# Four buffers of their own for the early modulation chunks, and a last norm on two engines instead of three

## What is computed

```python
h = jax.nn.gelu(einsum('tkd,td->tk', u, xx))      # PEER: all expert rows u against the tokens
mod = silu(c) @ w_ada + b_ada                      # 9 x 1024 modulation values, for x and for the context
x = x + 0.5 * g3x * swiglu(modulate(rmsnorm(x)), w13_ffn2, w2_ffn2)   # the last matmul is with w2_ffn2
return rmsnorm(x, norm_final)
```

## Time and profile before

| | us |
|---|---|
| median of 3 runs | 2147.66 (2146.67 to 2149.58) |
| the profiled execution: its own time | 2149.38 |
| its span in the profile | 2147.6 |
| PE busy in it | 2084.9 (97%) |
| DVE, ACT, POOL busy | 1233.9, 1037.9, 145.6 |
| mean DMA rate | 160 GB/s |

### The profile page before, as it was taken

How to read it: one execution, slowest core, us unless ns; L and a number is a source line. 1 busy time by engine, 2 the same in 40 slices (tenths; PEclk the granted TensorE clock), 3 DMA queues, 4 the chain that set the end, 5 groups by cost and what they waited for, 6 DMA issues and landing times.

```text
span 2147.6 us, 35688 instructions
## 1 busy us (share of the span) xinstructions
PE 2084.9 (97%) x12718; PEld 1820.1 (85%) x12718; DVE 1233.9 (57%) x2078; ACT 1037.9 (48%) x1585; POOL 145.6 (7%) x86
## 2 busy tenths in 40 slices
PE   8999999899999999999999999999999999999997
PEld 6899988668888888888888888887888898899996
DVE  5457895896666666666665333323655644356554
ACT  5645644675555555555554222213443444336763
POOL 1001667000000000000000000000000000000001
PEclk9999999999999999999999999999999999999999
DMA  5445456786655555565553223322333345354563
GB/s 203 152 131 174 148 206 216 256 309 209 192 191 186 186 189 188 190 205 186 189 165 106 93 95 97 108 97 83 97 100 118 101 145 176 100 186 144 177 197 117
DMA packets 95669, 343.97 MB, mean 160 GB/s; under 512 B 11011, under 2 KB 11523, under 8 KB 95333
## 3 DMA queue, kind: packets, MB, share of 16 engines
q1 hardware_dynamic: 94340, 337.28, 47.1%
q0 software_dynamic: 1248, 5.57, 0.8%
HBM read 341.76 MB, written 1.05 MB: 160 GB/s over the span
## 4 chain that ended last, share of the span: by engine, by line
PE 88%; DVE 4%; DMA 3%; ACT 2%; POOL 1%; issue 1%; SPq 0%; ACTq 0%; DVEq 0%; POOLq 0%
PE ps L1652 15%; PE ps L1653 15%; PE ps L1654 15%; PE ps L1911 8%; PE ps L1925 6%; PE ps L1927 5%; PE ps L1926 5%; PE ps L1913 4%; DMA RAW<-in_wstream 3%; PE ps L1685 2%; PE ps L1686 2%; PE ps L1687 2%; PE ps L1889 2%; POOL WL L458 1%; ACT WH L512 1%; PE ps L1847 1%
## 5 line engine op out<-in xcount | busy, mean ns | idle before, releaser
L993 DVE TENSOR_TENSOR WL<-RAW,WH 128x1024 fp32r<-128x1024 f32 x517 | 624.9, 1223 | 407.3 <-ACT WH L512 401.3
L512 ACT ACTIVATE WH<-RAW 128x1024 fp32r<-128x1024 f32 x565 | 585.5, 1053 | 280.2 <-PE ps L1927 106.7
L1652 PE MATMUL ps<-XH,WH 128*128 128x256 f32 (+1 forms) x1200 | 382.3, 319 | 6.0 <-DVE XL L1022 4.0
L1653 PE MATMUL ps<-XL,WH 128*128 128x256 f32 (+1 forms) x1200 | 379.1, 316 | 0.0
L1654 PE MATMUL ps<-XH,WL 128*128 128x256 f32 (+1 forms) x1200 | 379.1, 316 | 0.0
L1911 PE MATMUL ps<-XHL,WH 128*128 128x512 f32 x752 | 268.6, 397 | 0.0
L1652 PEld LDWEIGHTS ps<-XH,WH 128*128 128x128 f32 x1200 | 229.1, 191 | 24.7 <-DVE XL L1022 5.0
L1653 PEld LDWEIGHTS ps<-XL,WH 128*128 128x128 f32 x1200 | 229.3, 191 | 14.6
L1654 PEld LDWEIGHTS ps<-XH,WL 128*128 128x128 f32 x1200 | 229.2, 191 | 14.2
L1913 PE MATMUL ps<-XHL,WL 128*128 128x256 f32 x752 | 210.9, 280 | 0.0
L1925 PE MATMUL ps<-WH,AH 128*128 128x512 f32 x512 | 202.4, 395 | 0.0
(11 more groups left out here) (340 smaller groups left out, 3359.9 us busy)
## 6 DMA issues: line engine op xcount, KB each, us to landing
RAW<-in_wstream SPq DMA_DIRECT2D x637, 512.0 KB, 3.4
H<-in_xT SPq DMA_DIRECT2D x4, 256.0 KB, 6.1
CTX<-in_ctxT POOLq DMA_DIRECT2D x1, 1024.0 KB, 8.0
HX<-in_ctxT POOLq DMA_DIRECT2D x1, 1024.0 KB, 5.9
DIST<-in_dist POOLq DMA_DIRECT2D x1, 1024.0 KB, 5.4
out<-Y SPq DMA_DIRECT2D x4, 256.0 KB, 3.0
MASK<-in_mask POOLq DMA_DIRECT2D x1, 512.0 KB, 3.9
DFTL<-in_dftl POOLq DMA_DIRECT2D x1, 512.0 KB, 3.7
```

What stands on the lines that cost most here:

```text
L512: act.activation(WH[:, slot, :], RAW[:, slot, :], ACT.Copy).then_inc(hi_ready, 1)
L993: dve.tensor_tensor(WL[:, slot, :], RAW[:, slot, :], WH[:, slot, :].bitcast(F32), ALU.subtract).then_inc(lo_ready, 1)
L1652: pe.matmul(dst, wh, xh, start=start, stop=False, skip_group_check=not check)
L1653: pe.matmul(dst, wh, xl, start=False, stop=False, skip_group_check=not check)
```

## The change

The twelve early modulation chunks leave the stream and the ring. They stand at the end of the stream's array and are loaded into a buffer `ADB` of four slots in a free part of SBUF, with semaphores of their own. SP issues the first four with the loads of the stage before ("wq"), and the other eight with every second load of "pre"; `C_PRE` becomes contiguous.

The last four `down2` chunks are done for tile 0 first (chunk by chunk, both halves), then for tile 1 half 0 over the four chunks, then for tile 1 half 1. POOL's two steps of the last norm go to DVE, in a new order on DVE and ACT, and the fourth store is issued by ACT and not by SP.

```diff
-    ("ada", MODB),
+    ("ada", MODB - EARLY),
...
+C_PRE = range(C0["pre"], C0["pre"] + PRE)
+C_ADA = [None] * EARLY + list(range(C0["ada"], C0["peer"]))
...
+        ADB = sb("ADB", [P, 4, 1024])
...
+            def load_early(i):
+                if i >= 4:
+                    sp.wait_ge(s["early_used"], i - 3)
+                sp.dma_start(ADB[:, i % 4, :], a["wstream"][NCH + i]).then_inc(s[f"early_landed{i % 4}"], 16)
...
-            looped = C0["pre"] // 4
+            looped = C0["wq"] // 4
...
             for c in range(4 * looped, ADA_END):
-                if c in C_ADA:
+                if c >= C0["ada"]:
                     sp.wait_ge(chunk_done, c + 1)
                 else:
-                    sp.wait_ge(lo_ready, split_index(c) + 1)
+                    sp.wait_ge(lo_ready, c + 1)
                 load(c % 4, c + 4)
+                i = c - 4 * looped - 4
+                if 0 <= i < 4:
+                    if i == 0:
+                        sp.wait_ge(chunk_done, C0["wout"])
+                    load_early(i)
+                i = (c - C0["pre"] - 6) // 2 + 4
+                if (c - C0["pre"]) % 2 == 0 and 4 <= i < EARLY:
+                    load_early(i)
...
@@ mod_chunk (PE)
-                pe.wait_ge(landed[c % 4], 16 * (c // 4 + 1))
+                if i < EARLY:
+                    weights, used = ADB[:, i % 4, :], s["early_used"]
+                    pe.wait_ge(s[f"early_landed{i % 4}"], 16 * (i // 4 + 1))
+                else:
+                    weights, used = RAW[:, c % 4, :], chunk_done
+                    pe.wait_ge(landed[c % 4], 16 * (c // 4 + 1))
...
@@ down2 (PE)
             for k in range(FF):
-                c = C0["down2"] + k
-                split_ready(c)
+                split_ready(C0["down2"] + k)
                 pe.wait_ge(s["ffn_lo"], FF + k + 1)
-                for tt in range(TT):
+                for tt in range(TT if k < FF - 4 else 1):
                     for half in range(2):
...
-                if k < FF - 1:
+                        ins = down2(k, tt, half)
+                if k < FF - 4:
                     ins.then_inc(chunk_done, 1)
+            for half in range(2):
+                for k in range(FF - 4, FF):
+                    down2(k, 1, half)
...
@@ last norm (DVE)
             gated(0, 0)
+            added(0, 0)
             gated(0, 1)
+            added(0, 1)
+            dve.wait_ge(s["lastg_landed"], 16)
+            gain(0, 0)
+            half_mean(0)
+            gain(0, 1)
+            inverse(0)
             gated(1, 0)
-            added(0)
+            added(1, 0)
+            gain(1, 0)
+            half_mean(1)
             gated(1, 1)
-            added(1)
-            dve.wait_ge(s["lastg_landed"], 16)
-            half_mean(0)
-            half_mean(1)
-            gain(1)
-            inverse(0)
-            gain(0)
+            added(1, 1)
+            gain(1, 1)
             inverse(1)
...
@@ last norm (ACT)
             square(0, 0)
             square(0, 1)
             root(0)
+            scaled(0, 0)
+            scaled(0, 1)
             square(1, 0)
             square(1, 1)
             root(1)
-            scaled(0, 0)
-            scaled(0, 1)
             scaled(1, 0)
+            act.wait_ge(s["out_act"], 3)
+            act.dma_start(out[:, 1, 0:512], Y1[:, 1, 0:512]).then_inc(s["out_written"], 16)
```

More of the change, by code:

```diff
@@ L261, in build @@
         IOTA16 = sb("IOTA16", [P, TOPK], dt=U32)
+        ADB = sb("ADB", [P, 4, 1024])
+        assert place[0] <= REG + (PRE_ROW - 16) * 1024
         assert place[0] <= REG + PRE_ROW * 1024
@@ L359, in split_index @@
         def split_index(c):
-            return c - sum(a < c for a in C_ADA)
+            return c if c < C0["ada"] else c - (MODB - EARLY)
         def early_row(g):
@@ L410, in _ @@
             for c in range(4 * looped, ADA_END):
-                if c in C_ADA:
+                if c >= C0["ada"]:
                     sp.wait_ge(chunk_done, c + 1)
                 else:
-                    sp.wait_ge(lo_ready, split_index(c) + 1)
+                    sp.wait_ge(lo_ready, c + 1)
                 load(c % 4, c + 4)
+                i = c - 4 * looped - 4
[6 more added lines that the diff above has]
+                    load_early(i)
             with sp.Fori(0, (NCH - ADA_END - 4) // 4) as it:
                 for j in range(4):
-                    sp.wait_ge(lo_ready, at(ADA_END + 4 + j - 3 - MODB, 4, it))
+                    sp.wait_ge(lo_ready, at(split_index(ADA_END) + 4 + j - 3, 4, it))
                     load((ADA_END + 4 + j) % 4, it * 4 + (ADA_END + 4 + j))
-            for tt, half, ready, n in ((0, 0, "out_act", 1), (0, 1, "out_act", 2), (1, 1, "out_dve", 1), (1, 0, "out_act", 3)):
+            for tt, half, ready, n in ((0, 0, "out_act", 1), (0, 1, "out_act", 2), (1, 1, "out_dve", 1)):
                 d = slice(half * 512, half * 512 + 512)
@@ L489, in _ @@
             pool.dma_start(LASTG[:, :], a["lastg"]).then_inc(s["lastg_landed"], 16)
[L491 to L499, removed]
         @block.scalar
@@ L682, in _ @@
                     if i == AFTER[4 * g + 3] + 1:
-                        act.wait_ge(chunk_done, C_ADA[4 * g + 3] + 1)
+                        act.wait_ge(s["early_used"], 4 * g + 4)
                         act.activation(early_row(g), ps[:, 6 + g % 2, 0:256].rearrange("p (i j) -> p i j", i=2),
@@ L1601, in gated, with added, gain @@
                 dve.tensor_tensor(Y1[:, tt, d], ps[:, 4 + 2 * tt + half, :], G3B[:, d], ALU.mult).then_inc(s["y_gated"], 1)
-            def added(half):
+            def added(tt, half):
                 d = slice(half * 512, half * 512 + 512)
-                dve.wait_ge(s["y_gated"], half + 3)
-                dve.tensor_tensor(HXT[:, 1, d], Y1[:, 1, d], HXT[:, 1, d], ALU.add).then_inc(s["y_sum1"], 1)
-            def gain(half):
+                dve.wait_ge(s["y_gated"], 2 * tt + half + 1)
+                dve.tensor_tensor(HXT[:, tt, d], Y1[:, tt, d], HXT[:, tt, d], ALU.add).then_inc(s[f"y_sum{tt}"], 1)
+            def gain(tt, half):
                 d = slice(half * 512, half * 512 + 512)
-                dve.wait_ge(s["y_sum1"], half + 1)
-                dve.tensor_tensor(Y1[:, 1, d], HXT[:, 1, d], LASTG[:, d], ALU.mult).then_inc(s["y_gain1"], 1)
+                dve.wait_ge(s[f"y_sum{tt}"], half + 1)
+                dve.tensor_tensor(Y1[:, tt, d], HXT[:, tt, d], LASTG[:, d], ALU.mult).then_inc(s[f"y_gain{tt}"], 1)
             def half_mean(tt):
@@ L1846, in mod_chunk @@
                     rows, w0 = slice(32 * group, 32 * group + 32), kk * 512 + half * 256
-                    ins = pe.matmul(ps[rows, bank, 0:256], CS[:, 2 * (i % 4) + kk, :], RAW[:, c % 4, w0:w0 + 256],
+                    ins = pe.matmul(ps[rows, bank, 0:256], CS[:, 2 * (i % 4) + kk, :], weights[:, w0:w0 + 256],
                                     start=(i % 4 == 0), stop=(i % 4 == 3))
-                ins.then_inc(chunk_done, 1)
+                ins.then_inc(used, 1)
             def turn_row(g):
@@ L2152, in _, with down2 @@
             pe.wait_ge(s["hxt_dve"], 1)
+            def down2(k, tt, half):
+                c, t, d = C0["down2"] + k, slice(tt * P, tt * P + P), slice(half * 512, half * 512 + 512)
+                dst = ps[:, 4 + 2 * tt + half, :]
+                pe.matmul(dst, HIDH[:, k, t], WH[:, c % 4, d], start=(k == 0), stop=False)
+                pe.matmul(dst, HIDL[:, k, t], WH[:, c % 4, d], start=False, stop=False)
+                ins = pe.matmul(dst, HIDH[:, k, t], WL[:, c % 4, d], start=False, stop=(k == FF - 1))
+                if k == FF - 1:
+                    ins.then_inc(s["y_done"], 1)
+                return ins
             for k in range(FF):
-                c = C0["down2"] + k
-                split_ready(c)
+                split_ready(C0["down2"] + k)
                 pe.wait_ge(s["ffn_lo"], FF + k + 1)
-                for tt in range(TT):
+                for tt in range(TT if k < FF - 4 else 1):
                     for half in range(2):
[L2159 to L2165, removed]
-                if k < FF - 1:
+                        ins = down2(k, tt, half)
+                if k < FF - 4:
                     ins.then_inc(chunk_done, 1)
+            for half in range(2):
+                for k in range(FF - 4, FF):
+                    down2(k, 1, half)
 def lay_out(x):
@@ L2193, in lay_out @@
     ada = np.concatenate([tokens(x["w_ada_2"][0][:, n:n + 512]) for n in range(0, N_MOD * D, 512)], axis=0)
[L2194 to L2197, removed]
+    parts += [up[PRE_ROW:NKEYS], ada[EARLY:]]
     order = [up[0:1], up[1:2], down[PRE_ROW:NKEYS]]
@@ L2220, in lay_out @@
     parts += ffn(x["w13_ffn2_2"][0], x["w2_ffn2_2"][0])
+    parts += [ada[:EARLY]]
     stream = np.concatenate(parts, axis=0)
-    assert stream.shape == (NCH, P, 1024)
+    assert stream.shape == (NCH + EARLY, P, 1024)
     def acts(v):
```

## The result

The changed kernel takes 2137.66 us (median of 7 runs, 2132.96 to 2143.08), the kernel before 2147.66 (7 runs, 2142.46 to 2153.24). The ratio is 0.9944, 95% interval 0.9931 to 0.9958: by it 12.0 us less, from 9 to 15; the two medians differ by 10.0. Forecast were 2135.3 and 12.4 less. The profiled executions differ by more, 2147.6 to 2131.9, and the stages say why.

| stretch | before | after | change | forecast |
|---|---|---|---|---|
| start to the Gelu of expert chunk 0 | 270.7 | 272.8 | +2.2 | 0 |
| pre: Gelu of chunk 3 to that of chunk 31 | 97.9 | 90.6 | -7.4 | -8.3 |
| units: from there to the last `G<-ps` of the units | 111.0 | 104.9 | -6.1 | 0 |
| from there to the end of PE's last matmul | 1647.9 | 1647.8 | -0.1 | 0 |
| PE's last matmul to the end | 11.5 | 7.2 | -4.3 | -4.1 |

What follows compares the result with a forecast made beforehand. It took loads asked too late in pre, plus 11.5 us of norm and stores behind PE, as the bound. Early chunks 8.3 + end 4.1 = 12.4 us, from the median 2147.66 to 2135.3 us; range 2132.0 to 2140.5.

Steps and rivals of the forecast that it cites:

- The wait that bounds pre: In pre, loads are asked too late: SP's queue stands 51.3 us in 12 waits for modulation chunks.
- PE's own need, 88.0 us: Pre, Gelu of chunk 3 to 31: PE alone needs 88.0 us, took 97.9, so 9.9 are to be had.
- POOL and DVE, 1.6 us: In pre, POOL and DVE block each other during DVE's comparisons, taking 1.6 us off the 9.9 to be had.
- the two waits for POOL: In pre, PE would wait for POOL's low parts, 0.8 us at chunk 24 and 0.7 at chunk 26.
- The four first early loads past wq: They pass wq's loads in SP's queue; time to spare there, at worst 7.5 us once, not counted.
- The units stay: The stage of units starts in the same state, so its 113 us stay and the earlier gain reaches the end.
- Part B, 4.1 us: At the end, the new orders and ACT's store give 4.1 us; bounds 3.3 to 4.5.
- The mean's wait: At the end, DVE's mean waits for ACT's square, so the fourth gated step starts 0.45 us late.
- rival 1: POOL and DVE set pre: the early chunks' change gives 3 to 6 us there, total 2139; chance 0.26.
- 3: PE's waits in pre are POOL's and ACT's own chain; only the end gains, 2143.6; chance 0.06.
- 4: DMA can't move the 248 GB/s asked in pre; at 190 GB/s the time is 2155.6; chance 0.02.
- A: Early modulation chunks loaded into their own buffers: 8.3 us gained in pre, bounds 4.5 to 9.9.
- Rival 2: Everything in pre is hidden and the end gains more, 9.9 + 5.0 us, total 2132.8; chance 0.11.

Runs made afterwards that it cites:

- a_stand: Changed kernel with SP again waiting for modulation chunk n before its wait for the low part of expert chunk 4 + 2n; pre 90.5 us.
- a_short: Changed kernel with loads as late as in the old ring, the ring's places left free; pre 99.6 us, 2146.22 us in all (one execution).
- t_norm: Changed kernel with the new last norm but PE's old order of the last chunks; 11.3 us from PE's last matmul to the end.

## Why the prediction was right, and where it wasn't

- **The wait that bounds pre.** Right: the loads were late, not slow, and with buffers of their own the landings are no wait any more. The reason given for the lateness was not: "the time in which SP stands" costs nothing by itself (`a_stand`, 32.6 us of it); the loads came a chunk too late because the modulation chunks used up the ring's places ahead (`a_short`). The forecast wasn't hurt, since the change removes both.
- **PE's own need, 88.0 us.** Too small by 2.3: the term 12 x 0.57 is 12 x 0.76 = 9.1, as the rows of PE after show. With it the floor is 90.3, and 7.6 us were to be had, not 9.9.
- **POOL and DVE, 1.6 us.** Too large: PE lost 90.6 - 90.3 = 0.3, and neither of the two waits for POOL that were given as signs is there. (The two add up to 1.5, not 1.6.) DVE's comparisons after:

```profile
323.25 4.44 DVE L1265 TENSOR_TENSOR EQ<-IAU,IF 128x2048 uint32<-128x2048 uint32 x1
...
330.05 4.44 DVE L1265 TENSOR_TENSOR EQ<-IAU,IF 128x2048 uint32<-128x2048 uint32 x1
...
336.84 4.42 DVE L1265 TENSOR_TENSOR EQ<-IAU,IF 128x2048 uint32<-128x2048 uint32 x1
...
344.37 4.10 DVE L1272 TENSOR_TENSOR SEL<-VAL,GSUM 128x128 f32<-128x128 f32 x2
```

  Three of four take 4.4 us (two of four before), the sign that was named. But the selection ends at 348.5 and not at 356.0, earlier even than before (352.8), since other steps got shorter. The 16 additions of line 1213 in the trace before, in the trace after, and in `a_short`, where the line is 1216 (the lines view from 228 to 356):

```profile
L1213 DVE TENSOR_TENSOR CAND<-V 128x128 f32<-128x128 f32 (+1 forms) x16 | 15.9, 1039 | 0.0
...
L1213 DVE TENSOR_TENSOR CAND<-V 128x128 f32<-128x128 f32 (+1 forms) x16 | 6.8, 472 | 0.0
...
L1216 DVE TENSOR_TENSOR CAND<-V 128x128 f32<-128x128 f32 (+1 forms) x16 | 16.3, 1065 | 0.0
```

  They take 14.9 to 15.9 us in the four traces with the old ring and 6.7 to 6.9 in seven of the changed kernel and its variants; `a_short`, the changed kernel with late loads, is back at 16.3. `a_stand` and `t_norm` (loads in time, but no stretch of half clock in wq, see the next item) lie between, at 9.7 and 9.8. So most of it goes with when the loads come. Why was read and not isolated: with loads in time POOL's chunks come one by one with a gap (2.40 us, then 0.5 to 1.2 idle), with late ones often in pairs.
- **The four first early loads past wq.** No wait: ACT has none for a landing before pre, in either trace. But the trace after reaches chunk 0 2.2 us later. 1.5 of these are there before the first early load is issued (221.1), and so aren't its doing: the same `QT<-ps` of ACT starts at 216.7 before and 218.3 after, and the granted clock had been at half from 69 on for 3.4 us. The rest is in wq: from ACT's first `XHL` there (221.8 before, 223.3 after) to chunk 0 are 48.9 us before and 49.5 after, with the clock at half for 3.4 us from 236 on, behind a wait of 2.4 us of PE:

```profile
232.00:234.00 2.00, 0.27 (x3) 0.07 (x1) 2.00 (x3) 0.10 (x1) 1.19 (x1) 1.00 0.00 0
234.00:236.00 2.00, 1.35 (x11) 1.36 (x12) 1.70 (x9) 2.00 (x7) 0.00 (x0) 0.99 0.87 279
236.00:238.00 2.00, 2.00 (x12) 2.00 (x11) 1.90 (x15) 2.00 (x5) 1.35 (x1) 0.50 0.65 254
```

  PE waits these 2.4 us in the kernel before too, and the half clock behind them is in seven of the ten traces with the early loads and in none of the four without. The seven take 49.4 to 49.6 us there, all others 48.8 to 48.9. That the early loads bring it about is not shown; if they do, they cost 0.7 us.
- **The units stay.** Right in that nothing shows an effect; wrong in treating 113 us as a fixed length. One trace can't tell a stage's length when its loads land at times that vary from execution to execution.
- **Part B, 4.1 us.** 4.3 measured. The mean's wait held the fourth gated step 0.28 us instead of 0.45, and ACT's store landed within 3.0. (The prediction's "13 us that it doesn't work at the end" is a slip; its sum rightly uses 11.5.)
- **Rivals.** 1, 3 and 4 fell by the traces: no wait for POOL, 7.4 us of A there, 223 GB/s moved (near 250 expected). The total alone doesn't settle it: the median of 2137.66 lies nearer to rival 1 (2139) than to the forecast (2135.3), with runs that spread over 10 us. Rival 2 (all hidden) lies closest to the profiled run, 2133.7, but for another reason, the units.

So part of the hit was luck: of A's two errors one made the forecast gain 2.3 too large and the other 1.3 too small, and they nearly cancelled: 8.3 forecast, 7.4 measured.

## What to carry to other kernels

A ring's depth counts in chunks of every kind: chunks that are used as they come, without a split, take a place ahead from those that need the long way. Give them buffers of their own, or more places where slots are idle; ask for the distance from load to use in us, and not how long the queue stands. A new order of the matmuls and a new order of the steps behind them are worth less alone (2.1 and 0.2 us) than together (4.3): when the producer ends tile by tile, every consumer's queue must be in that order too. And where a few runs spread by 10 us, find the stage that spreads before comparing two traces.

## What the runs showed of the hardware

- Four matmul groups that write different 32 rows of the result take the time of one (0.57 against 0.54 us); between full matmuls such a chunk costs 0.76 us, 0.19 more than that.
- Loads of 512 KB land after 3.4 us (median, pre, trace after) to 5.4 (units, trace before), and in three executions of one kernel PE's waits for them in the units were 17.5, 8.9 and 6.8 us.
- The granted clock fell to half for 3.4 us behind a wait of 2.4 us of PE in seven of fourteen traces; the other seven have the same wait and kept the full clock.
- The comparison on DVE with two inputs took 2.29 us alone and 4.37 to 4.44 beside POOL's chunks. 16 smaller steps with two inputs took 6.8 us in all (9.7 in another trace) while POOL's chunks came one by one and 15.9 while they came in pairs, though POOL was busier in the first case (41.4 of 54 us against 36.6). That the spacing is the cause was read, not tested.
